# A woven two-stream transformer: another order of the context thread, high halves a slab ahead of low halves, norms in halves, one slab per attention turn, weighted values read from PSUM

## The chip, the cores and the metric

The kernel runs on one core of one Trainium2 chip. The metric is the device time of one execution in microseconds (us). Weights are streamed from HBM during the run; everything else stays in on-chip memory.

## What is computed

Two blocks stand behind one another, each of depth 2, for 256 latent tokens and 256 context tokens of width 1024, all in float32. The reference, cut to what matters:

```python
# first block, per layer l: x = latents, hctx = context, mc / ml = adaptive scales, shifts and gates
x = x + 0.5*gate * swiglu(ada_norm(x, ...), ffn_w_in[l,0], ffn_w_out[l,0])        # "ffn00", "ffn10"
x = x + gate * mixer(ada_norm(x, ...))      # l=0 "even": attention + mLSTM; l=1 "odd": gated linear attention
x = x + 0.5*gate * swiglu(ada_norm(x, ...), ffn_w_in[l,1], ffn_w_out[l,1])        # "ffn01", "ffn11"
# (the same for hctx; in layer 1 the context ends with the mixer's keys and values)
x = rms_norm(x, final_g)                                                           # "final"
# second block, i = 0: "mla" attention, i = 1: "na", a neighbourhood attention
h, hc = x*(1+sc1)+sh1, ctx*(1+csc1)+csh1                                           # "p00", "cp00", "p10", "cp10"
y, yc = mixer(h, hc)
x = _layer_norm(alpha*x + g1*y, ln1_g[i], ln1_b[i])                                # "ln00", "cln00", "ln10"
x = _layer_norm(alpha*x + g2*relu(h2 @ w1)**2 @ w2, ln2_g[i], ln2_b[i])            # "mlp0", "cmlp0", "mlp1"
# (the same for ctx, in i = 0 only: names that begin with c)
```

The adaptive scales come from `silu(c) @ ada_w + ada_b` for two condition vectors, one of the context and one of the latents.

## The kernel before

**Products in three terms.** A float32 product is made of three matmuls in the format fp32r: high x high, high x low, low x high (`products`, lines 2588 to 2596). So each weight slab (128 x 1024, 512 KB) goes through three steps: a DMA into `raw`, a rounding copy on ScalarE into `split_high` (line 1585), and on VectorE `raw - high` into `split_low` (line 2005), which overwrites `raw`. Activations are split in the same way: `h_high` on ScalarE, `h_low` on VectorE (line 2100), and `hidden_high`, `hidden_low` for the feed-forward layers. One slab feeds 24 matmuls of 256 columns (one stream) or 24 of 512 (both streams).

**One order for all engines.** `order()` (line 878) writes out by hand one list of steps, for instance `("up", f, h, ...)`, `("centre", tag, p)`, `("done", slab)`. `schedule()` (line 1064) turns each `done` into the fetch of the slab seven places on and the split of the slab five places on (`SLOTS, LAG = 7, 2`). Then each engine goes through the same list and carries out its own part of every step, in that order; semaphores do the rest. So what stands ahead of a step in the list stands ahead of it in the queue of every engine that has a part in both. A split is one step: ScalarE writes the high half, VectorE waits for it and writes the low half. `raw` and `low` share their memory, `high` has its own, seven buffers each.

**Threads.** Up to the end of the odd mixer both streams are multiplied together (512 columns). From there context and latents run as two threads that are woven: `beside_ffn11` (context mla beside the latents' ffn11), `beside_mla` (the latents' mla beside the context's mlp, "cmlp0"), `beside_mlp0` (the latents' mlp0, with the context's last norm cln01 and the projections of na), `na_steps`, then na_out, ln10, mlp1, ln11 and the store. `weave(pieces, groups)` yields one piece of products, then one group of other steps, in turns; `filled(groups, fill, n)` yields a group and then n pieces; `beside(units, pieces)` gives each attention turn one piece: the turn's steps, the late steps of the piece before (evictions and `done`), the products of the new piece, the scores of the turn.

**Norms.** A layer norm (`layer_norm_groups`, line 657) is: `mean_sum` (TensorE, over an accumulator that GpSimd adds up tile by tile, line 1463), `centre` of eight tiles (VectorE, line 2111, each followed by a square on ScalarE and an add on GpSimd), `sum` (TensorE, line 2646) and `mean` (VectorE, square root on ScalarE, reciprocal, line 2075), `rstd_spread` (TensorE, line 2612), `layer_norm` of eight tiles. `plain_tiles` then makes the scaled and shifted h: `plain` and `plain_put`, eight each, one group of 6 and one of 10.

**Adaptive scales.** 240 blocks of 128 outputs; from the seventh on, VectorE takes for each block two dot products over 1024 inputs, one per condition vector (`ada`, lines 2008 to 2021; the product is line 2019). They are spread over the feed-forward layers: 60 blocks each in ffn00, ffn01, ffn10 and 36 in mlp0. The blocks are loaded through SyncE's queue for odd n and through GpSimd's for even n (lines 1377 and 1450), each at its place in the list.

**Attention of the second block.** A turn u handles 128 queries of a pair of heads: scores in banks 0 to 2, maximum on VectorE, exponential on ScalarE, normalisation on VectorE, transpose by TensorE into banks 3 and 7, copy on ScalarE, and every second turn the weighted values (`mla_weigh`, `na_weigh`) in bank 6. ScalarE copies bank 6 to SBUF (lines 1787 and 1780), then writes the high half from there, and VectorE the low half. In `na_steps` the first five turns have a double piece each, one slab of keys and one of queries, in banks 4 and 5.

**mlp1** has all 32 hidden tiles at once: each of its eight `down` pieces uses four slabs, and the four `done` steps stand together behind the piece, after `add` (line 2208, `down_piece`, line 504).

## Time and profile before

| | |
|---|---|
| median of 3 runs | 3091.31 us (3087.28 to 3095.33) |
| the profiled execution | 3092.23 us, its span 3090.4 us |
| TensorE (PE) busy | 2881.0 us, 93% of the span, 17432 matmuls |
| VectorE (DVE) / ScalarE (ACT) / GpSimd (POOL) busy | 2090.8 / 1279.2 / 331.5 us |
| mean granted TensorE clock | 0.962 of full speed |
| DMA | 467.58 MB, mean 151 GB/s |

A busy TensorE is not TensorE at its peak, since the end of a matmul is modelled. What counts is the number of matmuls in a stretch, against the stretch's length, and the idle time in front of a matmul with what ended it.

### The profile page before, as it was taken

The page shows a single profiled execution, that of the slowest core. Times are in us where ns is not written, and L with a number is a line of the kernel's source. Part 1 is how long each engine was busy: PE and PEld are TensorE (multiplying, and loading weights), DVE is VectorE, ACT ScalarE, POOL GpSimd, SP SyncE. Part 2 cuts the span into 40 slices and gives each one's busy share as a digit, 9 for nine tenths or more (in the row PEclk, how much of TensorE's full clock was granted, in tenths as well). Part 3 has the DMA queues.
Part 4 walks back from the last instruction along what each step waited for, and adds up shares of the span by engine and source line. Part 5 has one row for each costly group of instructions (what it writes and reads, how often), then busy time and mean ns, then how long its engine had stood idle before and what let it go on. Part 6 is the DMA issues. An engine that isn't in the chain of part 4 may idle for free.

```text
span 3090.4 us, 43357 instructions
## 1 busy us (share of the span) xinstructions
PE 2881.0 (93%) x17432; PEld 2508.9 (81%) x17432; DVE 2090.8 (68%) x3510; ACT 1279.2 (41%) x2114; POOL 331.5 (11%) x380
## 2 busy tenths in 40 slices
PE   7999999888999999999999899899999798978998
PEld 6888897547888888888878888898799798966898
DVE  7799756555787857887557655665566799646664
ACT  4222244444322243222355654554555434535553
POOL 0000012222000010000111100221021101200100
PEclk8999999979999999999999999999999898989999
DMA  6666522102555535554322343444255675542453
GB/s 235 225 221 227 176 81 82 38 31 75 177 205 211 178 110 201 202 212 167 101 82 69 130 150 117 150 155 145 76 178 168 215 266 196 184 112 67 130 185 123
DMA packets 141142, 467.58 MB, mean 151 GB/s; under 512 B 26976, under 2 KB 29152, under 8 KB 140432
## 3 DMA queue, kind: packets, MB, share of 16 engines
q1 hardware_dynamic: 125392, 408.20, 39.6%
q0 software_dynamic: 15552, 56.63, 5.2%
q8 instruction: 138, 2.26, 0.3%
q14 instruction: 60, 0.49, 0.0%
HBM read 463.73 MB, written 1.05 MB: 150 GB/s over the span
## 4 chain that ended last, share of the span: by engine, by line
PE 74%; DVE 12%; ACT 8%; issue 3%; DMA 2%; POOL 1%; SPq 0%; ACTq 0%; DVEq 0%; POOLq 0%
PE bank L2593 22%; PE bank L2594 22%; PE bank L2595 22%; DVE sb_split_low L2005 3%; ACT sb_split_high L1585 2%; DVE sb_temp L2019 2%; POOL sb_temp L1463 1%; ACT sb_temp L1910 1%; PE bank L2881 1%; DVE sb_h_low L2092 1%; DMA sb_ada_mlp<-ada 1%; DVE sb_temp L2086 1%; DVE sb_x_res L2208 1%; PE bank L3028 1%; ACT sb_h_high L1656 1%
## 5 line engine op out<-in xcount | busy, mean ns | idle before, releaser
L2593 PE MATMUL bank<-sb_h_high,sb_split_high 128*128 128x256 f32 (+1 forms) x3392 | 1111.6, 328 | 66.2 <-DVE sb_h_low L2100 15.8
L2594 PE MATMUL bank<-sb_h_low,sb_split_high 128*128 128x256 f32 (+1 forms) x3392 | 1092.3, 322 | 0.0
L2595 PE MATMUL bank<-sb_h_high,sb_split_low 128*128 128x256 f32 (+1 forms) x3392 | 1091.7, 322 | 0.0
L2005 DVE TENSOR_TENSOR sb_split_low<-sb_raw,sb_split_high 128x1024 fp32r<-128x1024 f32 x620 | 758.3, 1227 | 267.4 <-ACT sb_split_high L1585 266.1
L1585 ACT ACTIVATE sb_split_high<-sb_raw 128x1024 fp32r<-128x1024 f32 x620 | 644.2, 1051 | 295.5 <-DMA sb_raw<-weights 295.2
L2593 PEld LDWEIGHTS bank<-sb_h_high,sb_split_high 128*128 128x128 f32 x3392 | 659.9, 195 | 131.1 <-DVE sb_h_low L2092 15.9
L2594 PEld LDWEIGHTS bank<-sb_h_low,sb_split_high 128*128 128x128 f32 x3392 | 660.9, 195 | 43.0
L2595 PEld LDWEIGHTS bank<-sb_h_high,sb_split_low 128*128 128x128 f32 x3392 | 660.2, 195 | 43.5
L2019 DVE CUSTOM_DVE_ANT_0 sb_temp<-sb_ada_ffn,sb_cond_ffn 128x1024 bf16<-128x1024 f32 x396 | 465.9, 1220 | 18.8 <-DMA sb_ada_ffn<-ada 10.3
L2593 PE MATMUL bank<-sb_hidden_high_ffn,sb_split_high 128*128 128x512 f32 (+1 forms) x830 | 281.8, 340 | 4.3 <-DVE sb_temp L2186 3.1
L2594 PE MATMUL bank<-sb_hidden_low_ffn,sb_split_high 128*128 128x512 f32 (+1 forms) x830 | 280.1, 338 | 0.0
L2595 PE MATMUL bank<-sb_hidden_high_ffn,sb_split_low 128*128 128x512 f32 (+1 forms) x830 | 280.1, 337 | 0.0
L2208 DVE SCALAR_TENSOR_TENSOR sb_x_res<-bank,sb_gates,sb_x_res 128x256 f32<-128x256 f32 x288 | 132.5, 479 | 152.8 <-PE bank L2595 146.2
L1688 ACT ACTIVATE sb_hidden_high_ffn<-sb_temp 128x512 fp32r<-128x512 f32 (+1 forms) x94 | 52.1, 555 | 344.4 <-DVE sb_temp L2186 344.4
L1675 ACT ACTIVATE sb_temp<-bank 128x256 f32<-128x256 f32 (+1 forms) x158 | 72.4, 458 | 281.5 <-PE bank L2595 281.3
L2593 PEld LDWEIGHTS bank<-sb_hidden_high_ffn,sb_split_high 128*128 128x128 f32 x830 | 157.3, 190 | 23.2 <-DVE sb_temp L2186 3.3
L2594 PEld LDWEIGHTS bank<-sb_hidden_low_ffn,sb_split_high 128*128 128x128 f32 x830 | 157.4, 190 | 18.6
L2595 PEld LDWEIGHTS bank<-sb_hidden_high_ffn,sb_split_low 128*128 128x128 f32 x830 | 157.3, 189 | 18.5
L2593 PE MATMUL bank<-sb_hidden_high_mlp,sb_split_high 128*128 128x256 f32 x512 | 148.2, 289 | 18.1 <-DVE sb_hidden_low_mlp L2198 17.6
L2594 PE MATMUL bank<-sb_hidden_low_mlp,sb_split_high 128*128 128x256 f32 x512 | 146.7, 287 | 0.0
L2595 PE MATMUL bank<-sb_hidden_high_mlp,sb_split_low 128*128 128x256 f32 x512 | 146.7, 287 | 0.0
L2186 DVE TENSOR_TENSOR sb_temp<-sb_temp,bank 128x512 f32<-128x512 f32 (+1 forms) x94 | 55.4, 590 | 133.1 <-PE bank L2595 133.1
(332 smaller groups left out, 3461.2 us busy)
## 6 DMA issues: line engine op xcount, KB each, us to landing
sb_raw<-weights SPq DMA_DIRECT2D x620, 512.0 KB, 3.4
sb_ada_ffn<-ada SPq DMA_DIRECT2D x114, 512.0 KB, 4.5
sb_ada_ffn<-ada POOLq DMA_DIRECT2D x90, 512.0 KB, 3.7
sb_ada_mlp<-ada POOLq DMA_DIRECT2D x18, 512.0 KB, 5.1
sb_ada_mlp<-ada SPq DMA_DIRECT2D x18, 512.0 KB, 5.0
sb_cond_ffn<-cond SPq DMA_DIRECT2D x3, 1024.0 KB, 5.3
sb_na_raw<-na_rpb SPq DMA_DIRECT2D x32, 96.0 KB, 6.0
sb_x_res<-tokens SPq DMA_DIRECT2D x4, 512.0 KB, 8.5
```

The costliest lines, as they stand in the source:

```text
L1463: do.tensor_tensor(acc, other if k == 1 else acc, new, ALU.add).then_inc(*pool.mark("added", (kind, tag, k, p)))
L1585: do.activation(m.high[s % SLOTS][:, :], m.raw[s % SLOTS][:, :], identity).then_inc(*act.mark("split_high", s))
L1656: do.activation(m.hh[:, k, COLS[p]], src, identity).then_inc(*act.mark("h_high", (tag, k, p)))
L1675: do.activation(m.hidden_temp(f, h, p), src, func).then_inc(*act.mark(name, (f, h, p)))
L1688: do.activation(m.hidden[f][i][:, m.hidden_cols(f, p)], m.hidden_temp(f, h, p), identity).then_inc(*act.mark("hidden_high", (f, h, p)))
L2005: do.tensor_tensor(m.low[i][:, :], m.raw[i][:, :], m.high[i][:, :].bitcast(F32), ALU.subtract).then_inc(*dve.mark("split_low", s))
L2019: do.tensor_tensor_reduce(out=m.junk(s), in0=m.ada[f][i][:, :], in1=m.cond[f][:, s, :], scale=1.0, scalar=0.0, op0=ALU.mult, op1=ALU.add, ...
L2186: do.tensor_tensor(temp, temp, src, ALU.mult).then_inc(*dve.mark("hidden_raw", (f, h, p)))
L2208: do.scalar_tensor_tensor(x, m.bank[bank][:, bank_cols(p, s)], m.gates_of(stage)[:, k, s:s + 1], x, ALU.mult, ALU.add).then_inc(*dve.mark( ...
L2593: do.matmul(out, ah, bh, start=start and j == 0, stop=False)
L2594: do.matmul(out, ah, bl, start=False, stop=False)
L2595: last = do.matmul(out, al, bh, start=False, stop=stop and j == len(terms) - 1)
```

## The change

It changes eight things together. (1) `raw` and `low` get eight buffers, `high` six; a slab's high half is still written five `done` steps ahead, its low half only four, and the two are separate steps; the high half also waits for the matmuls of the slab six places back. (2) Layer norms centre and scale in two halves of four tiles, with empty groups between, so that `sum` stands four groups behind `mean_sum`; the plain tiles come in groups of four. Where two fill pieces went with a group (ln00, ln01), one goes. cln01 is spread over twelve pieces of mlp0 instead of eight. (3) Behind odd_out, the norm n12 loses its four warming matmuls, and its `sum` comes after a first projection of the context. (4) Of 64 adaptive blocks (112 to 143, in ffn01, and 208 to 239, in mlp0) only the latents' dot product is taken; the context has no use for its own. All blocks are still loaded. (5) mla's weighted values of two heads share bank 6, and both halves are read from PSUM; VectorE's part (`weigh_put`) stands behind the turn's normalisation. (6) na has one slab per turn; its weighted values go straight into the context's half of h. (7) A `ready` step stands one piece later. (8) The result is stored in four parts of 256 KB.

The diff, cut to its core:

```diff
-SLOTS, LAG = 7, 2
+RAWS, HIGHS = 8, 6
...
-OUT_H = {"odd_out": CTX_PART}
+OUT_H = {"odd_out": CTX_PART, "na_out": CTX_PART}
...
+ADA_OF_LATENTS = ((72 + 5 * DT, 4 * DT), (192 + 2 * DT, 4 * DT))
...
         for k in range(DT - tail if last else DT):
+            body.append(down_piece(f, c, k, p, ring, last))
             if tail and last and k == DT - tail - 1:
                 body.append([("ready", down_slab(f, c, 8 * n - 1))])
-            body.append(down_piece(f, c, k, p, ring, last))
...
-WARM = {("n01", 1): (0, 5), ("n02", 1): (0, 9), ("n10", 1): (0, 5), ("n11", 1): (0, 5), ("n12", 1): (0, 4)}
+WARM = {("n01", 1): (0, 5), ("n02", 1): (0, 9), ("n10", 1): (0, 5), ("n11", 1): (0, 5)}
...
-    return [warm_sum(tag, p, 0) + [("mean_sum", tag, p), ("centre", tag, p)], [], warm_sum(tag, p, 1) + [("sum", tag, p), ("mean", tag, p)],
-            [("rstd_spread", tag, p), ("layer_norm", tag, p)]]
+    first, second = range(0, 4), range(4, DT)
+    return [[], [("mean_sum", tag, p), ("centre", tag, p, first)], [("centre", tag, p, second)], [], [], [("sum", tag, p), ("mean", tag, p)],
+            [("rstd_spread", tag, p), ("layer_norm", tag, p, first)], [("layer_norm", tag, p, second)]]
...
-    return layer_norm_groups(tag, p) + in_groups(plain_tiles(plain, p), (6,))
+    return layer_norm_groups(tag, p) + in_groups(plain_tiles(plain, p), (4, 4, 4) if tag not in NEAR_NORMS else (6,))
...
+        if i > 2 and (i - 2) % per == 0:
+            turn += [("weigh_put", kind, 2 * ((i - 2) // per) - 2), ("weigh_put", kind, 2 * ((i - 2) // per) - 1)]
...
-    for j in range(3):
+    for j in range(4):
         yield from fm_piece("na_k", j, LAT_PART, ring)
         yield from fm_piece("na_q", j, LAT_PART, ring)
...
-    pieces = [both(fm_piece("na_k", j, LAT_PART, ring), fm_piece("na_q", j, LAT_PART, ring)) for j in range(3, 8)]
-    pieces += [*tm_pieces("na_v1", ring), None, None]
+    pieces = [fm_piece(name, j, LAT_PART, ring) for j in range(4, 8) for name in ("na_k", "na_q")]
+    pieces += tm_pieces("na_v1", ring)
...
-    norm = ada_norm_groups("n12", 1)
-    yield from norm[0]
+    sums, spread, *tiles = ada_norm_groups("n12", 1)
     yield from late
-    yield from down[0]
-    yield from weave(norm[1:], down[1:4])
+    yield from weave(down[:6], [sums, [], spread, *tiles])
...
-    yield from filled(layer_and_plain_groups("ln00", "p01", 1), fill, 2)
+    yield from filled(layer_and_plain_groups("ln00", "p01", 1), fill)
...
-    yield from weave(pieces[:8], [[], [], *layer_norm_groups("cln01", 0)])
+    yield from weave(pieces[:12], [[], *layer_norm_groups("cln01", 0)])
...
-    n_split = 0
+    n_high = n_low = HIGHS - 1
     for step in order():
...
+        s = PLACE[step[1]]
+        if step[0] == "done" and s + RAWS < N_SLABS:
+            yield "fetch", s + RAWS
+        ahead = HIGHS - 1 if step[0] == "done" else 0
+        while n_high <= min(s + ahead, N_SLABS - 1):
+            yield "split_high", n_high
+            n_high += 1
+        while n_low <= min(s + max(ahead - 1, 0), N_SLABS - 1):
+            yield "split_low", n_low
+            n_low += 1
...
-        for k in range(DT):
+        for k in range(0, DT, 2):
             wait_for_x(sp, "ln11", k, LAT_PART)
-        do.dma_start(m.out, m.x[:, :, LAT]).then_inc(*sp.mark("stored", "all", step=16))
+            wait_for_x(sp, "ln11", k + 1, LAT_PART)
+            do.dma_start(m.out[:, k:k + 2, :], m.x[:, k:k + 2, LAT]).then_inc(*sp.mark("stored", "all", step=16))
...
+        if s >= HIGHS:
+            act.wait_ge("gemm", s - HIGHS)
+        do.activation(m.high[s % HIGHS][:, :], m.raw[s % RAWS][:, :], identity).then_inc(*act.mark("split_high", s))
...
-            y = m.fm_tile("mla", MLA_QN + hd, p)
-            do.activation(y, m.bank[6][:, 0:NC_TOK], identity).then_inc(*act.mark("weigh_copy", (kind, hd)))
-            act.wait_ge("weigh_copy", (kind, hd))
-            put_high(of(p, "mla_y"), hd, p, y)
+            act.wait_ge("weighed", (kind, hd // 2 * 2 + 1))
+            put_high(of(p, "mla_y"), hd, p, m.weighed(hd))
...
-        for s in range(2):
-            if n > BLOCKS:
+        for s in streams_of_ada(n):
+            if n > BLOCKS and s in streams_of_ada(n - 1):
                 dve.wait_ge("ada_dot", (n - 1, s))
```

## Rows read from the trace of the kernel before

**Rows 1.** The page: busy time of each engine, share of the span, instructions

```profile
PE 2881.0 (93%) x17432; PEld 2508.9 (81%) x17432; DVE 2090.8 (68%) x3510; ACT 1279.2 (41%) x2114; POOL 331.5 (11%) x380
```

**Rows 2.** Stretches: length; PE, PEld, DVE, ACT, POOL busy (count); clock, DMA share, GB/s

```profile
1200.00:1250.00 50.00, 50.00 (x220) 41.13 (x219) 40.19 (x61) 15.59 (x19) 2.65 (x5) 1.00 0.60 204
1710.00:1750.00 40.00, 33.63 (x239) 31.96 (x240) 26.28 (x51) 25.43 (x48) 14.54 (x15) 0.91 0.32 106
1930.00:1985.00 55.00, 45.83 (x345) 44.50 (x345) 34.62 (x61) 33.80 (x59) 21.36 (x22) 0.94 0.42 137
2050.00:2090.00 40.00, 33.66 (x240) 32.88 (x239) 24.27 (x43) 21.79 (x40) 11.23 (x11) 0.87 0.37 127
2275.00:2345.00 70.00, 60.62 (x487) 59.43 (x486) 45.70 (x77) 42.98 (x73) 16.18 (x18) 0.98 0.45 150
2398.00:2633.00 235.00, 199.52 (x1552) 197.07 (x1550) 205.39 (x337) 99.92 (x162) 26.12 (x33) 0.91 0.65 225
...
2683.00:2874.00 191.00, 155.22 (x1070) 131.78 (x1068) 113.33 (x211) 79.59 (x154) 3.26 (x5) 0.92 0.39 106
2895.00:3074.00 179.00, 179.00 (x1510) 178.95 (x1508) 101.76 (x142) 83.16 (x129) 4.44 (x6) 1.00 0.52 168
```

**Rows 3.** What TensorE waited for in the whole span: us, times, longest

```profile
PE bank L2646 <- POOL sb_temp L1463: 21.7, 9, 9.5
PE bank L2593 <- DVE sb_hidden_low_mlp L2198: 17.6, 7, 3.5
PE bank L2593 <- DVE sb_na_k_lat L2218: 16.4, 3, 7.5
...
PE bank L2862 <- ACT sb_mla_ctx L1787: 5.0, 4, 2.7
...
PE bank L2862 <- ACT sb_mla_lat L1787: 2.7, 4, 0.7
```

**Rows 4.** VectorE by line in mlp0 (2400 to 2632 us): count, busy, mean ns, idle before

```profile
L2019 DVE CUSTOM_DVE_ANT_0 sb_temp<-sb_ada_mlp,sb_cond_mlp 128x1024 bf16<-128x1024 f32 x72 | 85.1, 1220 | 8.2 <-DMA sb_ada_mlp<-ada 8.2
```

**Rows 5.** Start of mlp0 in order of time: start, us, engine, line, idle before

```profile
2415.16 2.74 DVE L2111 SCALAR_TENSOR_TENSOR sb_x_res<-bank,sb_x_res 128x256 f32<-128x256 f32 x8
...
2419.55 3.33 POOL L1463 TENSOR_TENSOR sb_temp<-sb_temp,sb_square 128x256 f32<-128x256 f32 x4
...
2422.93 1.02 PE L2646 MATMUL bank<-sb_const,sb_temp 128*128 128x1 f32 x4 [9.51 <-POOL sb_temp L1463]
...
2427.97 1.22 DVE L2019 CUSTOM_DVE_ANT_0 sb_temp<-sb_ada_mlp,sb_cond_mlp 128x1024 bf16<-128x1024 f32 x1 [5.59 <-DMA sb_ada_mlp<-ada]
...
2436.47 1.22 PE L2612 MATMUL bank<-sb_const,sb_stat 128*128 128x128 f32 x4 [7.70 <-DVE sb_stat L2075]
```

**Rows 6.** Stretches of na: the five double turns, the turns after them

```profile
2716.00:2783.00 67.00, 45.71 (x300) 39.88 (x298) 32.56 (x59) 21.60 (x41) 0.00 (x0) 0.85 0.40 99
2783.00:2857.00 74.00, 60.70 (x422) 45.89 (x422) 50.32 (x107) 39.00 (x90) 0.00 (x0) 0.93 0.28 68
```

**Rows 7.** VectorE behind a down piece of mlp1, in order of time

```profile
3051.91 0.48 DVE L2208 SCALAR_TENSOR_TENSOR sb_x_res<-bank,sb_gates,sb_x_res 128x256 f32<-128x256 f32 x1 [5.01 <-PE bank L2595]
3052.31 4.62 DVE L2005 TENSOR_TENSOR sb_split_low<-sb_raw,sb_split_high 128x1024 fp32r<-128x1024 f32 x4
```

**Rows 8.** Two equal waits of TensorE, and the stretch behind each

```profile
1949.68 0.80 PE L2679 MATMUL bank<-sb_temp,sb_const 128*128 128x256 f32 x2 [2.29 <-POOL sb_temp L1463]
...
2278.89 0.70 PE L2679 MATMUL bank<-sb_temp,sb_const 128*128 128x256 f32 x2 [2.29 <-POOL sb_temp L1463]
...
1950.00:1957.00 7.00, 7.00 (x47) 6.92 (x45) 2.74 (x8) 3.07 (x9) 3.98 (x6) 0.76 0.19 68
2279.00:2286.00 7.00, 7.00 (x58) 6.95 (x59) 3.23 (x9) 2.93 (x8) 3.86 (x6) 1.00 0.31 97
```

**Rows 9.** DMA issues of the page: count, KB each, median us to landing; the store in its window

```profile
sb_raw<-weights SPq DMA_DIRECT2D x620, 512.0 KB, 3.4
...
out<-sb_x_res SPq DMA_DIRECT2D x1, 1024.0 KB, 4.8
```

More of the change, by code:

```diff
@@ L680, in beside @@
         late = [step for step in piece if step[0] not in PRODUCTS]
+        if any(step[0] == "tm_copy" and step[1] == "na_v1" for step in late):
+            yield from late
+            late = []
         yield from first
@@ L872, in na_steps @@
         units[2 * t - 1][0].append(("na_bias", t))
-    units[11][0].extend(("na_put", k) for k in range(4))
-    yield from beside(units, pieces)
+    yield from beside(units[:18], pieces)
+    last, _ = units[18]
+    yield from last
     yield from flat(pieces)
@@ L906, in order @@
     yield "scales", "n00"
-    yield "split", 0
+    yield "split_low", 0
     yield "mods", 0, BLOCKS
     first, *tiles = ada_norm_groups("n00", 0)
-    yield from weave([[("split", s)] for s in range(1, SLOTS - LAG)], tiles)
+    yield from weave([[("split_low", s)] for s in range(1, HIGHS - 1)], tiles)
     first, *tiles = ada_norm_groups("n00", 1)
@@ L991, in beside_ffn11 @@
     ring = Ring(0, 4)
[L992 removed]
+    yield from filled([[], down[6]], body)
     yield from mla_front(CTX_PART, ring, body)
@@ L1304, in chunk_of, with streams_of_ada @@
     return max(c for c in range(len(SIZES[f])) if chunk_at(f, c) <= h)
+def streams_of_ada(n):
+    return (1,) if any(first <= n < first + count for first, count in ADA_OF_LATENTS) else (0, 1)
 def ada_stage(n):
```

130 lines of the change are left out of this document (57 added, 73 removed).

## The prediction

> **What bounds the kernel now.** I read the page first. TensorE is busy for 93% of the span [rows 1], so the first guess is TensorE. The stretches say where that holds, and where its granted clock is full. With both streams in one product TensorE has no gap at all, at clock 1.00 (the first stretch of [rows 2]): there an edit for VectorE earns nothing. The same holds in mlp1 (the last stretch of [rows 2]), which also gives the pace of one stream: 179.00 us for 1510 matmuls, 0.1185 us each, 2.84 us for a slab of 24. In the woven part between, the same count takes longer. I price each stretch as its length less 0.1185 us times its matmuls (in order [rows 2]): odd_out and n12 11.7 us too long (40 - 28.3), cln00 14.1, the final norm and p00 11.6, ln00 12.3, mlp0 51.1 (235 - 183.9). For na the form of the matmuls differs, so it is worked out by turns below. The list of TensorE's waits gives the causes [rows 3]: sums that wait for GpSimd's additions (21.7 us), hidden_low in mlp0 (17.6), evictions of na's keys (16.4), and the copies of weighted values (5.0 and 2.7). In mlp0 VectorE is the engine that is full: 205.39 of 235 us [rows 2].
>
> **mlp0, part 4 of the change.** VectorE makes 72 dot products of 1.22 us there [rows 4]. 32 of them go, 32 x 1.22 = 39 us, and VectorE's 205 us become 166, below TensorE's 184: the waits for hidden_low go almost wholly. The 32 in ffn01 earn nothing, since TensorE is full in that kind of stretch [rows 2]. But the start is another matter. mean_sum is followed by eight centrings, squares, and additions of some 0.83 us a tile on GpSimd (3.33 us for 4) [rows 5]; `sum` waited 9.51 us for them. Behind them in GpSimd's queue stands the load of a next adaptive block, so VectorE waited 5.59 us for that DMA, and the spread 7.70 us for VectorE [rows 5]. Now four tiles come ahead of that load and four behind it. The first half is done by about 2419, the load lands some 5 us later, VectorE then has two dot products and two splits before the second half, and `sum` can run at about 2431, when TensorE has been waiting since 2419: a wait of 12 and then one of 2, against 9.5 and 7.7, but with two slabs (5.7 us) more done. So the start gives back only 4 us or so (bounds -3 and 17, all of it). Of the 51 us I take 26 back: 17.6 of waits, about 4 at the start, and 4 of low clock behind them; bounds 10 and 45. All loads remain, 225 GB/s on the mean [rows 2].
>
> **na, part 6.** With a double piece in banks 4 and 5, the next double piece needs both banks, and their evictions stand in VectorE's queue behind the turn's maximum and normalisation. That is the wait on sb_na_k_lat [rows 3]. With one slab a turn, the bank that a piece needs was left two turns earlier. The double turns take 67 us for five [rows 6], 13.4 each; the ten slabs are 28.4 of the 45.71 us that TensorE is busy, which leaves 17.3, some 3.0 to 3.5 for a turn's own matmuls, so 9 a turn would do. Ten slabs of keys and queries are now two ahead and eight in eight turns. VectorE's 32.56 us make 6.5 a double turn; less one split and one eviction, some 1.6, that is 4.9. TensorE has 2.84 + 3.0: I take 5.8. Later turns take 74 us for fourteen, 5.3 each [rows 6]; these keep about their pace. New: 34 us ahead of the turns (8 slabs and v0), 46 for eight turns, 27 for four with v1, 21 and 15 for the last seven, 3 and 13 for what is left of na_out: 159, against 191 [rows 2]. I take 31 back; bounds 14 and 39.
>
> **The norms, parts 2 and 3.** In each of the four stretches the excess is waits on bursts (eight centrings, ten plain tiles in a row) and the clock behind them. `sum` four pieces behind mean_sum is 11.4 us, more than eight additions take. A spread one piece behind its `sum` was still waited for in cln00 and now can be in ln00 and ln01. I take back 5 of 11.7 at n12 (whose four warming matmuls and a wait go, while the wait for the last tiles of cp00 now shows), 9 of 14.1, 8 of 11.6, 8 of 12.3, and 2 for ln01 and ln10 together: 32; bounds 10 and 46.
>
> **Weighted values, part 5.** The two waits go: 5.0 + 2.7 [rows 3], 8 us; bounds 4 and 10 (VectorE's reads of PSUM, which stand in the normalisation's lee).
>
> **Store, part 8.** 1024 KB land in 4.8 us, 512 KB in 3.4 [rows 9]. The last part of 256 KB cannot take longer than the 512: at least 1.4 us less; the straight line gives 2.0, which I take. The worst is 0. The Trainium skill, "DMA: Bandwidth & Descriptors", section "Anatomy of one DMA", gives a fixed cost of about 2.0 us per DMA plus bytes over 436 GB/s: an estimate of 2.6 us for the last part if the four overlap, and of 10.4 if they follow one another, which would turn the 2 us of gain into a loss of some 3. No row of the trace before shows four stores in a row.
>
> **What the split of the splits costs, part 1.** A slab's low half is now made at the `done` four places before it. Where each piece ends one slab, that leaves three slabs of time. In mlp1 a down piece ends four slabs at once, and all four `done` steps stand behind `add`, which waits for the piece's last matmul. So the low half of the next piece's first slab is made only then: 0.40 us from add to the first split and 4.62/4 = 1.16 for it [rows 7], at least 1.6. Two signals come to that, of 0.05 us at the least (the additions end at 2422.88, the sum starts at 2422.93 [rows 5]); with a third of a microsecond for both, 1.9 us of waiting at seven piece borders (the first is fed by the ups), 13 us. The clock: of two equal waits of 2.29 us one was followed by 0.76 over 7 us, which is 0.24 x 7 = 1.7 us lost to time at 1.2 instead of 2.4 GHz, the other by 1.00, full speed [rows 8]. I count it at two of seven, 4 us: 17 us lost, bounds 12 and 26. Elsewhere VectorE is spared waiting for the high half of the same slab; I count the gain as nothing and let the range have it, with the new wait of ScalarE for the slab six back (long done where it is asked). The later `ready` is covered by a piece of products. The Trainium skill, "TensorE: Matmul & The Clock Gate", section "HAM oscillation", has a kernel whose wait in every step of a loop put the array back on half clock every time; by it the clock would be paid at all seven borders.
>
> **The sum.** Back: 26 + 31 + 32 + 8 + 2 = 99. Lost: 17, and 8 for waits that come in place of those removed (VectorE's 166 of 184 us in mlp0 leave it little room), bounds 0 and 25. Net 74. The profiled execution took 3092.2, 0.9 above the median of the runs, so 3092.2 - 74 = 3018.
>
> **Rivals.** (a) The forecast, 3018, own range 3000 to 3034: 0.40. (b) The clock falls at every border of mlp1: 7 x 1.7 = 12 instead of 4, so 3026. For it stands the first pair of [rows 8], against it the second: 0.10. (c) The chains, not the bursts, set the pace: in mlp0 the loads (GpSimd's block behind the additions) keep VectorE waiting and only 10 come back, in na the turn is bound by maximum, exponential, normalisation at some 7 us instead of 5.8, and 15 come back; 3018 + 16 + 16 = 3050. For it: 5.59 us of waiting on a load [rows 5] and turns of 5.3 with little more than half a slab in each [rows 6]. 0.22. (d) The waits go wholly: mlp0 gives 45, na 37, the norms 38, nothing comes in their place: 3018 - 19 - 6 - 6 = 2987, or 2979 with the 8. For it: VectorE has room in every woven stretch but mlp0 [rows 2]. 0.18. (e) Slower: the later low halves reach TensorE late in the whole woven part, not in mlp1 alone. The place is VectorE's queue wherever it runs more than three slabs behind; the price is one slab, 2.84 us, at each such place; it decides from (99 - 17)/2.84 = 29 places on; with 35 of them it gives 3092 - 99 + 17 + 99 = 3109. Against it: VectorE is busy for about two thirds of most of these stretches [rows 2]. 0.04. (f) The gains are there but each is eaten by the next wait, and little is left, 3085 to 3100: 0.06, the rest.
>
> **How the numbers follow.** 0.3%, some 9 us, is about what a measurement of this kernel can tell from no change. Faster by more than that takes (a) to (d) and a sliver of (f): 0.91; within: 0.05; slower: 0.04. The range goes from the near end of (d) to beyond (c), 2986 to 3060, and leaves out about 2 in 10.
>
> **What would show it.** In the changed profile: mlp0's stretch near 209 us for its 1552 matmuls, with line 2019's successor at 40 dot products and no wait for hidden_low above 2 us; `sum` of cln01 still waiting some 10 us; na's stretch near 160; no wait of a weigh for its copy; in mlp1 seven waits on sb_split_low of 1.9 us and 192 to 196 us for the 1510 matmuls. I would be wrong in the mechanism if mlp1 showed no such waits, or if VectorE were still full in mlp0.

## The result, and the profile after

The changed kernel takes 2977.0 us (median of four runs, 2976.8 to 2977.8) against 3090.7 for the kernel before: a ratio of 0.963 with a 95% interval of 0.9615 to 0.9648, 114 us less. My forecast was 3018, and 2977 lies below the low end of my range, 2986. The direction was right and the size wrong, by 41 us. Two of four later runs of the changed kernel, at 3502 and 3504 us and a granted clock of 0.74, were in a slower state and count nowhere below.

The busy times of the page, TensorE first (busy, share, instructions), and below them VectorE and ScalarE:

```profile
PE 2838.8 (95%) x17424; PEld 2478.5 (83%) x17424; DVE 2010.1 (68%) x3382; ACT 1275.3 (43%) x2092; POOL 338.6 (11%) x380
```

VectorE did 80.7 us less (64 dot products of 1.22 us are 78 of them). TensorE's busy time fell by 42 us with only 8 matmuls fewer [rows 1]. Most of that is clock: the mean granted clock over the span rose from 0.962 to 0.978, and what the low clock took from TensorE while it was busy fell from 88.8 to 52.4 us. Its idle time in front of matmuls fell from 197.8 to 126.7 us.

The stretches, with the columns of [rows 2], cut so that each holds about as many matmuls as before: n12, cln00, the final norm and p00, ln00, mlp0, na and mlp1.

```profile
1702.00:1738.00 36.00, 30.77 (x237) 30.15 (x238) 25.22 (x46) 23.63 (x45) 13.92 (x15) 0.95 0.37 126
1904.00:1948.00 44.00, 41.67 (x342) 40.98 (x341) 30.83 (x53) 27.66 (x48) 17.08 (x17) 1.00 0.52 171
2013.00:2044.00 31.00, 29.55 (x244) 28.94 (x243) 22.02 (x42) 19.99 (x39) 9.55 (x10) 1.00 0.49 165
2216.00:2283.00 67.00, 61.60 (x504) 60.33 (x503) 47.26 (x83) 42.87 (x73) 22.38 (x22) 1.00 0.49 164
2336.00:2541.00 205.00, 189.17 (x1553) 188.41 (x1552) 168.79 (x272) 100.84 (x162) 26.37 (x33) 0.96 0.72 258
2590.00:2746.00 156.00, 144.46 (x1054) 123.79 (x1054) 111.60 (x210) 75.12 (x144) 1.99 (x3) 0.97 0.48 126
2767.00:2961.00 194.00, 181.76 (x1510) 180.33 (x1510) 102.74 (x143) 86.16 (x129) 4.43 (x6) 1.00 0.45 152
```

By the pace of [rows 2], 0.1185 us a matmul, the excess is 7.9, 3.5, 2.1 and 7.3 us in the four norm stretches (11.7, 14.1, 11.6, 12.3 before), 21.0 in mlp0 (51.1), and in mlp1 it is 15.1 where there was none. The granted clock is at 1.00 in three of the six woven stretches (all but mlp1); before it was in none.

TensorE's waits in the whole span (us in total, times, longest):

```profile
PE bank L2601 <- DVE sb_split_low L2015: 15.0, 9, 2.0
PE bank L2654 <- POOL sb_temp L1483: 14.8, 6, 12.2
PE bank L2601 <- DVE sb_h_low L2110: 13.0, 10, 2.5
PE bank L2638 <- DMA sb_ada_ffn<-ada: 12.9, 3, 9.2
PE bank L2620 <- DVE sb_stat L2085: 8.1, 5, 3.2
...
PE bank L2601 <- DVE sb_hidden_low_mlp L2208: 0.4, 1, 0.4
```

Of the rows that led my list [rows 3], hidden_low went from 17.6 to 0.4, sb_na_k_lat and both copies of weighted values are gone, and the wait for GpSimd's additions went from 21.7 to 14.8, nearly all of it one wait of 12.2. The new first row is sb_split_low, and seven of its nine waits lie in mlp1.

What I had misjudged shows in another row: VectorE's own waits. The first row is of the page of before and is not among those that the prediction uses; the second answers to it in the changed kernel (count, busy, mean ns, then VectorE's idle time just before and what ended it).

```profile
L2005 DVE TENSOR_TENSOR sb_split_low<-sb_raw,sb_split_high 128x1024 fp32r<-128x1024 f32 x620 | 758.3, 1227 | 267.4 <-ACT sb_split_high L1585 266.1
```

```profile
L2015 DVE TENSOR_TENSOR sb_split_low<-sb_raw,sb_split_high 128x1024 fp32r<-128x1024 f32 x620 | 758.3, 1232 | 13.6 <-ACT sb_split_high L1603 13.6
```

VectorE stood 266 us, in 230 waits, with a low half next in its queue, waiting for ScalarE to make the high half of the very same slab. Now it is 13.6. Everything queued behind (evictions, additions, norms) stood there with it. The idle time as such did not go: VectorE is idle for 965 us of the span against 1000 before, and its waits for TensorE's results grew (the largest two rows from 165.7 and 133.1 to 206.6 and 200.8). What changed is what it waits for.

To place the gain in time I matched the two traces by the weight products (15,594 in each, in the same order but for a few pieces) and took the difference of the time between equal counts. In us less than before: up to 1703 us of the changed kernel 7.6; odd_out and n12 5.2; ffn11 with mla's context half 13.6; cln00 10.7; final norm and p00 9.9; mla's latent half 9.4; ln00 5.3; mlp0 32.7; ln01 and cna -1.0; na 34.6; mlp1 -14.9; the tail after the last product 2.2. The sum is 115.3, the difference of the two spans (3090.4 and 2975.1).

### The profile page after: what moved, and what is told of

The parts are those of the page before. It is cut to its first block and busy times, and to the rows that moved or that the text cites. A ratio compares the mean times of both kernels' runs of the same rounds, so it can differ in the third digit from the quotient of the medians.

```text
span 2975.1 us, 43424 instructions
## 1 busy us (share of the span) xinstructions
PE 2838.8 (95%) x17424; PEld 2478.5 (83%) x17424; DVE 2010.1 (68%) x3382; ACT 1275.3 (43%) x2092; POOL 338.6 (11%) x380
## 5 line engine op out<-in xcount | busy, mean ns | idle before, releaser
L2015 DVE TENSOR_TENSOR sb_split_low<-sb_raw,sb_split_high 128x1024 fp32r<-128x1024 f32 x620 | 758.3, 1232 | 13.6 <-ACT sb_split_high L1603 13.6
L2029 DVE CUSTOM_DVE_ANT_0 sb_temp<-sb_ada_ffn,sb_cond_ffn 128x1024 bf16<-128x1024 f32 x364 | 429.6, 1219 | 24.0 <-DMA sb_ada_ffn<-ada 15.3
L2196 DVE TENSOR_TENSOR sb_temp<-sb_temp,bank 128x512 f32<-128x512 f32 (+1 forms) x94 | 55.5, 590 | 202.3 <-PE bank L2603 200.8
L2601 PE MATMUL bank<-sb_hidden_high_mlp,sb_split_high 128*128 128x256 f32 x512 | 144.2, 282 | 12.6 <-DVE sb_split_low L2015 12.2
L1461 POOL DMA_DIRECT2D sb_ada_ffn<-ada x90 | 47.8, 531 | 844.0 <-DVE sb_ada_col L2029 844.0
```

The source lines that it names most:

```text
L1461: lane.do.dma_start(m.ada[f][i][:, :], m.w["ada"][n, :, :]).then_inc(*lane.mark(ada_signal(n), n, step=16))
L2015: do.tensor_tensor(m.low[i][:, :], m.raw[i][:, :], m.high[s % HIGHS][:, :].bitcast(F32), ALU.subtract).then_inc(*dve.mark("split_low", s))
L2029: do.tensor_tensor_reduce(out=m.junk(s), in0=m.ada[f][i][:, :], in1=m.cond[f][:, s, :], scale=1.0, scalar=0.0, op0=ALU.mult, op1=ALU.add, ...
L2196: do.tensor_tensor(temp, temp, src, ALU.mult).then_inc(*dve.mark("hidden_raw", (f, h, p)))
L2601: do.matmul(out, ah, bh, start=start and j == 0, stop=False)
```

## The experiments

Unless said otherwise each kernel is the changed one with the edit shown, its time a median of four runs, and "against the changed kernel" means against 2977.0. "Stage" figures are read from the one profiled execution of each kernel, matched by weight products as above, so they need not add up to the difference of the medians: the profiled run was the fastest of four for before_staggered (3063.9) and the slowest for done_before_add (2964.4) and all_dots (3003.2). Part of the scatter between kernels is not the edit's: more on that at one_store.

**The low half beside the high half (low_beside_high).**

```diff
-        while n_low <= min(s + max(ahead - 1, 0), N_SLABS - 1):
+        while n_low <= min(s + ahead, N_SLABS - 1):
```

> The changed kernel with one edit: the low half of a slab is made at the same `done` as its high half, five places ahead, as before the change; the eight raw buffers stay. Measured so far: 2977.0 us for the changed kernel; mlp1 took 15 us longer than before, with seven waits on sb_split_low of up to 1.9 us (12.2 in all), and the two attention stages of mla took some 27 us less than before, of which my prediction priced 7.7. Theory A: the order of the splits is what costs in mlp1 (the low halves behind `add`) and what gains in mla (the lone split_low waits of 3.6 and 2.6 us there, and the clock behind them): then mlp1 gives 15 us back, mla loses some 10 to 15, and the whole is 2970 to 2980. Theory B: the gain in mla comes from the weighted values read from PSUM and has nothing to do with the splits: then mla stays, mlp1 gives 15 back, and the whole is 2962 to 2966. Theory C (rival): the seven waits come from the buffers and not from the order; then they stay and the whole is 2977.

3001.9 us (ratio to before 0.9713, 0.9698 to 0.9727): 24.9 more. mlp1 got its 14.9 back and has no such wait; all else lost 39 us by stage (up to n12 10.1, of which 6.3 ahead of odd_out, where both streams are multiplied together; mla's context half 7.8; cln00 3.7; final norm 2.1; mla's latent half 1.7; ln00 4.2; mlp0 2.5; na 6.7; the rest small). VectorE's waits:

```profile
DVE sb_split_low L2015 <- ACT sb_split_high L1603: 269.9, 244, 7.9
```

The waiting is back whole, so it is the order that makes it. TensorE's idle time is 138.2 us against 126.7, although the 12.2 of mlp1 are gone: 24 of the 39 us are idle time, and the rest is busy time at the same matmuls, that is mostly clock (0.972 against 0.978). None of my three theories had the sum: A had mlp1 right and mla nearly (9.5 us lost in its two halves, 10 to 15 said), but not the 30 us that other stages lost. B and C are wrong.

How such a wait reaches TensorE is seen in the kernel before, at 1797 us (start, us, engine, idle before):

```profile
1796.82 1.99 ACT L1585 ACTIVATE sb_split_high<-sb_raw 128x1024 fp32r<-128x1024 f32 x2
...
1797.90 1.23 DVE L2005 TENSOR_TENSOR sb_split_low<-sb_raw,sb_split_high 128x1024 fp32r<-128x1024 f32 x1 [0.79 <-ACT sb_split_high L1585]
1799.04 0.75 DVE L2478 COPY sb_mla_kv<-bank 128x256 f32<-128x256 f32 x2
1799.56 0.36 PE L2593 MATMUL bank<-sb_h_high,sb_split_high 128*128 128x256 f32 x1 [3.55 <-DVE sb_split_low L2005]
```

ScalarE was late with two slabs, VectorE waited 0.79 us for the first, and TensorE, whose next matmul needed that slab, waited 3.55 us until its low half was made (it ended at 1799.12).

**Part 1 alone on the kernel before (before_staggered).** Seven buffers as before, high halves five places ahead, low four. The diff is cut to its core.

```diff
-            last = step[1] + (SLOTS - LAG if step[0] == "done" else 0)
-            while n_split <= min(last, N_SLABS - 1):
+            ahead = SLOTS - LAG if step[0] == "done" else 0
+            while n_high <= min(step[1] + ahead, N_SLABS - 1):
+                yield "split_high", n_high
+                n_high += 1
+            while n_split <= min(step[1] + max(ahead - 1, 0), N_SLABS - 1):
...
```

> The kernel before with one part of the change alone: ScalarE makes the high half five places ahead, VectorE the low half four places ahead, in the seven buffers it has. My prediction priced this part at 17 us lost (mlp1's seven borders) and nothing gained: 3108 by it. Theory A: the part is worth the same on the old schedule as undoing it cost on the new one, 24.9 us net (40 gained where both streams' work is woven, 15 lost in mlp1): 3064 to 3069. Rival B: the other parts are what leaves VectorE the room to profit; in mlp0, where it is busy 205 of 235 us, and at the bursts of the norms the freed waiting is filled at once: 3075 to 3095. Rival C: on the old schedule, where VectorE's waits stall TensorE more often, it is worth more than 25: 3050 to 3063.

3066.3 us (ratio 0.9921, 0.9906 to 0.9936), 24.0 less than the 3090.3 of the kernel before in the same sitting. That is theory A: the part is worth about the same on either schedule. That 24.0 and 24.9 agree to 1 us is luck, since each is good to 3 to 5. In the profiled execution, 28.6 us shorter than that of the kernel before, mlp1 loses 17.4 us and all else gains 46, 9 of them ahead of odd_out and 7.4 in mlp0, where undoing the part on the new schedule cost only 2.5. VectorE's waits for high halves are 13.9 us here.

**The order or the eighth buffer (seven_staggered).** `RAWS, HIGHS = 7, 7`, high halves still five ahead, low four.

> The changed kernel with the buffers of before (seven raw, seven high) and its new order of the splits (high five places ahead, low four). Measured so far: with the low half beside the high one and eight raw buffers 3001.9, 24.9 us more than the changed kernel; all stages but mlp1 lose some 40 us together, mlp1 gains 14.9; VectorE waits 270 us for ScalarE's high halves there (266 before the change), 13.6 in the changed kernel. Theory A: it is the order alone, since VectorE no longer stands behind ScalarE: then this kernel is 2977, at most 2980. Rival B: a part of it is the eighth raw buffer, which lets a load start one slab earlier; then the raw tiles are late in places, and the time lies between 2980 and 3000, with waits of sb_split_high on the DMA.

2980.5 us (2977.4 to 2982.8), 3.5 more, with no stage more than 2.6 longer. VectorE waits 13.9 us for high halves, as in the changed kernel. ScalarE now waits for the loads of the raw slabs, as B has it, but nobody waits for ScalarE (idle before, and what ended it):

```profile
L1603 ACT ACTIVATE sb_split_high<-sb_raw 128x1024 fp32r<-128x1024 f32 x620 | 646.8, 1051 | 322.0 <-DMA sb_raw<-weights 317.0 <-PE bank L2603 5.0
```

It is the order; the eighth raw buffer, and six `high` buffers instead of seven, bring nothing that these runs resolve.

**The low halves ahead of `add` (done_before_add).**

```diff
-    steps = [("down", f, c, k, p, bank), ("add", f, (f, c, k), k, p, bank), *part_done(f, p, *done)]
+    steps = [("down", f, c, k, p, bank), *part_done(f, p, *done[:-1]), ("add", f, (f, c, k), k, p, bank), *part_done(f, p, *done[-1:])]
```

> The changed kernel with one edit: in a down piece that ends four slabs, the first three `done` steps stand ahead of `add`, so that VectorE makes those low halves while TensorE is still in the piece. If the low half behind `add` is the cause of the seven waits in mlp1, they go (12.2 us) and with them the low clock behind some of them, 15 us in all, while everything else stays: 2962 (2960 to 2965). If the cause is that four slabs of weights end at once and the fetches or the high halves are late, the waits stay and the time is 2977. A loss is possible where the add of another kernel stage is now held up behind a split that waits for its high half: then 2980 or more, with new waits on sb_x_res.

2960.7 us (ratio 0.958, 0.9566 to 0.9595), 16.3 less, nearly all of it in mlp1 (14.9 by stage). First a border of mlp1 in the changed kernel (the first one: the addition, the low halves behind it and TensorE's wait), then the same border here.

```profile
2867.08 0.48 DVE L2218 SCALAR_TENSOR_TENSOR sb_x_res<-bank,sb_gates,sb_x_res 128x256 f32<-128x256 f32 x1 [8.38 <-PE bank L2603]
2867.48 4.62 DVE L2015 TENSOR_TENSOR sb_split_low<-sb_raw,sb_split_high 128x1024 fp32r<-128x1024 f32 x4
...
2868.85 0.36 PE L2601 MATMUL bank<-sb_hidden_high_mlp,sb_split_high 128*128 128x256 f32 x1 [1.80 <-DVE sb_split_low L2015]
```

```profile
2859.91 4.62 DVE L2015 TENSOR_TENSOR sb_split_low<-sb_raw,sb_split_high 128x1024 fp32r<-128x1024 f32 x4
2869.51 0.48 DVE L2218 SCALAR_TENSOR_TENSOR sb_x_res<-bank,sb_gates,sb_x_res 128x256 f32<-128x256 f32 x1 [4.98 <-PE bank L2603]
```

There VectorE sits idle 8.38 us and then makes four halves in a row, too late for the first. Here three of them are made in that idle time (the first of the four in the row is that of the slab before, due there in both kernels), and TensorE has no wait on sb_split_low in all of mlp1. The cause at the borders is shown, and this is the first kernel that beats both.

**Weighted values copied again, in mla (weigh_copies).** ScalarE copies them to sb_mla_ctx and sb_mla_lat, both reads come from there, and each head has the whole bank to itself again; VectorE's part stays at its new place, behind the turn's normalisation.

> The changed kernel with the weighted values of mla copied by ScalarE to sb_mla_ctx or sb_mla_lat and read from there, as before the change (na keeps reading PSUM). Theory A, by my prediction's term: the waits of the weigh products for the copies come back, 5.0 + 2.7 us, and the whole is 2984 to 2986. Theory B: those waits were also what put the clock down behind them and what held the low splits back; then all that the two mla stages gained beyond the order of the splits comes back, 15 to 27 us, and the whole is 2992 to 3004. Rival: the copies were waited for only because VectorE's part stood at another place of the turn; with the puts at the end of the turn nothing comes back and it is 2977 to 2980.

2987.2 us, 10.1 more: 4.3 and 3.6 in mla's two halves, the rest spread. The waits for the copies are back as two rows:

```profile
PE bank L2871 <- ACT sb_mla_ctx L1799: 3.5, 4, 1.2
PE bank L2871 <- ACT sb_mla_lat L1799: 2.7, 4, 0.7
```

My term, 8, holds; theory B does not: the mla stages gained 23.0 and this part is 7.9 of it.

**All dot products (all_dots).** `ADA_OF_LATENTS = ()`: 64 more, whose results nothing uses.

> The changed kernel with the dot products of the adaptive blocks made for both streams again (32 more in ffn01, 32 more in mlp0; what they write is not used). mlp0 took some 210 us against 235 before, all but 15.4 us of waits of its first blocks gone. Theory A (mine): VectorE's time in mlp0 goes from 166 to 205 us beside 184 us of TensorE, the waits for hidden_low come back, and mlp0 takes 15 to 22 us more, ffn01 nothing: 2992 to 2999. Rival: the later splits or the spread norms were what freed mlp0, and the 64 products cost little: 2977 to 2982. Second rival: ffn01 also pays, since the low halves are now made later: 3005 or more.

2999.0 us, 21.9 more; mlp0 takes 23.4 more by stage, every other stage 1.7 or less, ffn01 0.0, so the 32 products dropped there earned nothing, as forecast. mlp0's stretch is this, and its waits on hidden_low are back (9.5 us, 6 times):

```profile
2336.00:2564.00 228.00, 197.82 (x1551) 194.25 (x1549) 203.70 (x336) 99.96 (x163) 26.03 (x32) 0.93 0.66 231
```

VectorE is at 204 of 228 us again and the clock at 0.93 instead of 0.96. TensorE's idle time grew by 14 of the 23 us and its busy time by 8.7 (197.82 against 189.17); the latter goes with the clock.

**Two slabs a turn in na (na_double).** Three of eight keys and queries ahead, then `both(...)` for five, and two empty places, as before.

> The changed kernel with na's keys and queries two slabs a turn again (three of eight ahead, five double pieces in banks 4 and 5). The stretch of na became 34.6 us shorter with the change, of which the run with the low halves beside the high ones gave 6.7 back. Theory A (mine): the pairing in two banks cost the rest, by evictions that stand behind the turn's normalisation: then 22 to 30 us come back, all in na: 2999 to 3007, with waits on sb_na_k_lat of some 15 us. Rival: most of it was the low halves and the weighted values, and the pairing costs only the 3 to 10 us that the waits' excess over a turn makes: 2980 to 2987.

3003.9 us, 26.9 more; 22.2 of it in na, 4.2 in mlp0, which the edit does not touch. The row of before is back:

```profile
PE bank L2601 <- DVE sb_na_k_lat L2228: 16.6, 3, 7.7
PE bank L2601 <- ACT sb_na_k_lat L1718: 4.9, 2, 3.2
```

The weighted values of na, which also lost their copy with the change, were tried in no run.

**The norms whole and early (norms_whole).** One centring and one normalisation a norm, `sum` two groups behind, plain tiles in sixes, two pieces a group in ln00 and ln01; the final norm in one part, p00 in fours as before.

> The changed kernel with the norms of the woven stretches in one part each and early, as before (cln00, cln01, ln00, ln01, the final norm and p00; n12 keeps its new order). Measured gains of these stages: cln00 10.7, final norm and p00 9.9, ln00 5.3, mlp0 32.7, of which the late low halves give 3.7, 2.1, 4.2 and 2.5 and the dot products of mlp0 23.4. Theory A: what is left is the norms': 7.0 + 7.8 + 1.1 + 6.8 = 23, so 2997 to 3002. Rival B: the parts are not separate; without the freed VectorE the bursts cost more, now they cost less, and only 8 to 15 come back: 2985 to 2992. In both the mlp0 part would be a wait of the spread for VectorE (7.7 us before).

2996.6 us, 19.5 more: cln00 6.8, final norm and p00 8.1, mla's latent half 2.8, mlp0 4.2, ln00 0.1, ln01 with cna -1.0. Just short of theory A (2997 to 3002), far from B. The spread of cln01 waits 7.9 us for VectorE again (7.7 before).

**One store (one_store), the same once more (one_store_again), and the changed kernel once more (after_again).**

```diff
-        for k in range(0, DT, 2):
+        for k in range(DT):
             wait_for_x(sp, "ln11", k, LAT_PART)
-            wait_for_x(sp, "ln11", k + 1, LAT_PART)
-            do.dma_start(m.out[:, k:k + 2, :], m.x[:, k:k + 2, LAT]).then_inc(*sp.mark("stored", "all", step=16))
+        do.dma_start(m.out, m.x[:, :, LAT]).then_inc(*sp.mark("stored", "all", step=16))
```

> The changed kernel with one store of all eight tiles at the end, as before the change. From the last product of weights to the end of the span it was 16.2 us before and 14.1 with four stores. If the four stores are what made that difference, it is 16.2 again and the time 2979; if the norm's end is what became shorter, it stays at 14.1 and the time at 2977.

> The kernel with one store once more. Theory A (scatter between sittings): anywhere from 2977 to 2988, and not with the same extra time in mlp0, cna, na and mlp1. Theory B (its own time, by the clock's answer to the same waits): 2985 to 2988 again, with the same stages longer. The tail is 16.3 us in both.

> The changed kernel once more, unchanged. Theory A: the 6.8 us that one_store lost outside its tail are scatter between one placing of the program and the next, or between hours on the chip: then this run may lie anywhere from 2974 to 2985. Theory B: a program's time is its own to 1 us: then 2976 to 2978.

2986.6 us, then 2981.7 in another sitting; the changed kernel came to 2976.2 and 2973.7 in that sitting (two runs; ratio 0.9628, 0.9609 to 0.9647). From the last weight product to the end of the span it is 16.3 us with one store and 14.1 with four: 2.2 us, the only thing that the edit can reach. The other 7 us of the first sitting lie in mlp0 (1.4), cna (1.7), na (1.6) and mlp1 (2.7). mlp1 there has the same seven waits, 12.2 us in all, but the clock stands at 0.98, not 1.00:

```profile
2774.00:2970.00 196.00, 183.77 (x1496) 182.10 (x1496) 102.55 (x144) 84.87 (x127) 4.44 (x6) 0.98 0.45 148
```

Ten of the profiles have these seven waits, 12.2 us in all each time. Behind them the granted clock fell to half in none of the seven in three profiles (the changed kernel, one_store_again, norms_whole), in one in three (after_again, na_double, all_dots) and in two in four (one_store, seven_staggered, before_staggered, weigh_copies): 11 falls for 70 waits, each 1.7 us lost, and mlp1's 1505 weight products take 193.5 to 196.8 us with it. One of the falls, in one_store:

```profile
2874.00:2877.00 3.00, 3.00 (x16) 3.00 (x15) 2.22 (x2) 0.00 (x0) 0.00 (x0) 0.50 0.00 0
```

So the same schedule gives times that differ by some 5 us between sittings, in part by the clock's answer to equal waits, and single runs of one kernel in one sitting differ by up to 9 us (2950.6 to 2960.0 for sum_later_sp). A single term above is good to 3 to 5 us and not better; the 3.5 of seven_staggered is inside that.

**The start of mlp0.** cln01's `sum` waits 12.2 us. The rows say why: GpSimd adds the first squares, then issues a block's load, VectorE waits for that block, and the second four tiles are behind it.

```profile
2357.06 0.57 POOL L1461 DMA_DIRECT2D sb_ada_mlp<-ada  x1
...
2361.59 1.23 DVE L2029 CUSTOM_DVE_ANT_0 sb_temp<-sb_ada_mlp,sb_cond_mlp 128x1024 bf16<-128x1024 f32 x1 [5.13 <-DMA sb_ada_mlp<-ada]
...
2369.68 1.01 PE L2654 MATMUL bank<-sb_const,sb_temp 128*128 128x1 f32 x4 [12.24 <-POOL sb_temp L1483]
```

Five kernels, all with the early low halves (alone 2960.7), take it up. The waits given are TensorE's.

sp_loads_early_done, all adaptive blocks loaded by SyncE and none by GpSimd:

> Two edits to the changed kernel: the first three `done` steps of a down piece ahead of `add` (alone: 2960.7 us, mlp1's seven waits gone), and all adaptive blocks loaded by SyncE, none by GpSimd. In cln01 `sum` waits 12.2 us for GpSimd's additions and the spread 3.2 for VectorE, because GpSimd issues a block's load behind its first additions and VectorE waits 5.1 us for that block ahead of the second centring. Theory A: without that load the second half of the norm comes some 5 to 6 us earlier, and 5 to 9 us are gained: 2952 to 2956. Rival B: VectorE's own queue (dot products and splits between the halves) sets the place of `sum`; then nothing is gained, 2959 to 2961. Rival C: SyncE's queue, with loads waiting for a free block, holds the weights' loads back: then the raw tiles are late and the time is 2965 or more.

2958.0 us; the wait of `sum` is 7.5.

sum_later, `sum` three pieces later:

> Two edits to the changed kernel: the early `done` steps of the down pieces (alone 2960.7) and, in cln01 beside mlp0, `sum` and all behind it three pieces later; GpSimd goes on loading its blocks. Three more pieces are 3 to 6 us of products ahead of `sum`, so the wait of 12.3 us for GpSimd's additions shrinks to some 6 to 9 and, if the clock fell in it, a little more comes back: theory A 2953 to 2957. Rival B: the products in the added pieces themselves wait for VectorE, whose queue is what is late (hidden_low); then the wait only changes its name and the time is 2959 to 2962.

2959.5 us; the wait for the additions is gone, and 11.4 us on sb_split_low, 8.3 of them at one place, stand in its place.

sum_later_sp, both:

> The same with all adaptive blocks loaded by SyncE (with the early `done` steps and SyncE's loads, without the later `sum`: 2958.0, the wait for the additions 7.5 us). Theory A: three pieces more take 3 to 6 us of those 7.5, and the spread's 3 to 4 us shrink too: 2950 to 2954. Rival B, as above: VectorE's queue is late and the wait changes its name: 2957 to 2960.

2952.9 us (2950.6 to 2960.0; ratio 0.9558, 0.9543 to 0.9573); mlp0 takes 4.0 less by stage than in the changed kernel, and 8.2 us of waiting on sb_split_low remain, 4.8 of them at one place.

loads_ahead, each block of mlp0 loaded four blocks ahead of its dot product, by the engine that loads it now:

```diff
+def loads_at(n):
+    first, count = FFN["mlp0"][1:3]
+    if n < first:
+        return [n]
+    early = [n, n + 2] if n < first + 2 else []
+    return early + [n + 4] * (n + 4 < first + count)
...
-            load_ada(m, pool, n)
+            for at in loads_at(n):
+                load_ada(m, pool, at)
```

> Two edits: the early `done` steps (alone 2960.7) and, in mlp0, the load of an adaptive block issued four blocks ahead of its dot product instead of at its place, on the same engines. In the changed kernel VectorE waits 5.1 us for a block's load ahead of the second centring, the load having been issued behind GpSimd's additions and 3.6 us away from its data. Theory A: that wait goes, the second half of the centrings comes 4 to 5 us earlier, `sum` waits 7 to 8 instead of 12.3, and VectorE keeps up in the rest of mlp0: 2953 to 2957. Rival B: GpSimd's eight additions and ScalarE's squares set `sum`'s place, the load is hidden: 2959 to 2962. Rival C: earlier loads hold SyncE or GpSimd in a wait for a free block, and weights come late: over 2965.

2957.7 us; the wait is 7.9, mlp0 takes 3.8 less by stage, and VectorE's wait for blocks fell from 21.6 us, 13 times, to 2.3, twice:

```profile
PE bank L2664 <- POOL sb_temp L1493: 7.9, 1, 7.9
PE bank L2630 <- DVE sb_stat L2095: 4.2, 1, 4.2
DVE sb_temp L2039 <- DMA sb_ada_mlp<-ada: 2.3, 2, 2.0
```

loads_ahead_later, with `sum` three pieces later:

> The same with `sum` three pieces later (with the early `done` steps alone 2959.5, where the wait had moved to sb_split_low, 8.3 us at one place, since VectorE stood waiting for a block's load). Theory A: with the loads ahead VectorE doesn't stand, the 8.3 us at sb_split_low go to 0 to 2, and the `sum` wait stays away: 2946 to 2951, faster than all so far. Rival B: the wait for VectorE stays wherever it is put, since VectorE has more work at the start of mlp0 than TensorE: 2956 to 2960.

2954.5 us (2950.6 to 2957.1; ratio 0.9561, 0.9547 to 0.9575); 7.6 us of waiting on sb_split_low, where theory A said 0 to 2.

So the load accounts for some 4 to 5 us of the 12.2. The rest did not go with it: put `sum` later, and the wait takes another name. That this rest is VectorE's and GpSimd's own work at that place is the likely reading, and no run takes such work away there. All five kernels lie within 7 us of each other, near the scatter; sum_later_sp and loads_ahead_later are the fastest, some 23 us below the changed kernel, and I don't rank them. Of those 23 us, 16 are those of done_before_add.

## Why the prediction was wrong

**The step that failed.** It is in "What the split of the splits costs": "Elsewhere VectorE is spared waiting for the high half of the same slab; I count the gain as nothing and let the range have it." That part, priced at 17 lost, measured 24 to 25 gained, on both schedules: 39 back by stage on the new one (33 of them where work is woven, 6 ahead of it), against 15 lost in mlp1. What I put at nothing without a number was the largest term of all, and my bounds for the part, 12 to 26 lost, had no gain in them either. The error of this one step, 42 us, is as large as the whole miss (41). The other parts were 17 too high together (99 against the 82 that undoing them one by one gives), and the 8 for new waits and 7 that no single part shows offset 15 of that. The row that points to it stood on the page of before: 266 us of VectorE waiting for ScalarE. I read TensorE's waits and VectorE's busy share and saw room at two thirds busy; but while an engine stands in front of one step, nothing behind that step is done, however little the engine is busy. The row gives the place and not the price:

```profile
DVE sb_split_low L2005 <- ACT sb_split_high L1585: 155.3, 139, 5.2
```

That is the woven part of the kernel before, from 1703 to 2895 us, where 33 us came back; 94.0 us of such waits lie ahead of it, where 6 came back (9 on the old schedule). The price has to be sought in TensorE's own waits that end with VectorE's work: in the woven part of the list of before sb_h_low has 15.8 + 1.6, sb_ctx_temp 8.8 and sb_split_low 6.1, 32 us, and there is the clock behind them. That is a size to start from, not a bound.

**mlp1's borders: right, to a tenth.** Forecast: seven waits on sb_split_low of 1.9 us, 13 us, stretch 192 to 196. Found: 12.2 in seven (six of 1.8 to 1.9, one of 1.4), stretch 194. The clock term was 4 (two of seven borders); ten profiles had none to two falls, 1.1 on the mean, of the 1.7 us that I had priced. The changed kernel's own profile has none, and still 2.9 us remain beside the waits (15.1 - 12.2). 1.7 of them lie at the same borders, for which I had no term: at six of them, from the last matmul's start before the wait to the first one's behind it are 2.08 to 2.14 us, and then 0.19 to the next, where the pace is 0.12, so each border costs 0.24 more than the idle time shown. Rival (b), a fall at every border, is wrong. The Trainium skill, "TensorE: Matmul & The Clock Gate", section "HAM oscillation", tells of a kernel where a wait at every step put the array back on half clock each time. Those waits were longer, some 3 to 5 us by the page, and I should not have carried the effect over to waits of 1.9; here the clock fell at 11 of 70 borders.

**mlp0: 26 forecast, 32.7 by stage, 30 by stretch** (205 us for 1553 matmuls; I had said 209). VectorE is at 168.8 us (166 said), 40 dot products, hidden_low 0.4. At the start I said a wait of 12 and one of 2: it was 12.2 and 3.2, for the reasons given. The dot products alone are 22 to 23. TensorE's busy time fell by 10.4 us (199.52 to 189.17) as the clock rose from 0.91 to 0.96, where my term was 4.

**na: 31 forecast, 34.6**, 156 us (160 said); the pairing alone is 22 to 27 by na_double, and 6.7 of the stage are the splits'. The other 5.7 no run takes apart.

**The norms: 32 forecast, 31.1 minus 1.0 by stage** (n12 5.2 for 5, cln00 10.7 for 9, final norm 9.9 for 8, ln00 5.3 for 8, ln01 and cna -1.0 for 2). But the sum is right by offset: norms_whole gives only 19.5 for this part. Some 14 us of these stages (3.8 + 3.7 + 2.1 + 4.2) belong to the splits. I had read the excess of a stretch and given all of what could go to the norms in it. n12's new order was not tried alone; what is left for it is 5.2 - 3.8.

**Weighted values: 8 forecast, 10.1** (7.9 in mla). The mla stages gained 23.0 in all; the other 15 I had nowhere. Undone one at a time, the splits' order gives 9.5 of them and the norms 2.8.

**Store: 2.0 forecast, 2.2.** Each of the four parts landed 2.6 us after its issue, and they were issued within 3.4 us, so they overlap:

```profile
out<-sb_x_res SPq DMA_DIRECT2D x4, 256.0 KB, 2.6
```

By the Trainium skill, "DMA: Bandwidth & Descriptors", section "Anatomy of one DMA", the estimate was 2.6 us for one part; the trace agrees, though the section gives its fit for DMAs that GpSimd issues and SyncE issues these.

**"8 for waits that come in place of those removed"**: little of it came. Beside the waits forecast in mlp1 and cln01, the largest that the list of before does not have are in na: 2.4 us on sb_na_q, and 5.8 on an exponential (sb_temp L1920), where it was 3.6.

**Before the woven part** I forecast nothing and 7.6 us came. 6.3 us of it went again with the low halves beside the high ones, and the order alone gave 9 on the old schedule, though 3 us of such figures are inside the scatter that the last stretch of it shows (3.2 us between two profiles of the changed kernel).

**Do the parts add up?** Undone one at a time: 24.9 + 26.9 + 19.5 + 21.9 + 10.1 + 2.2, and 1.4 for n12, are 107 of 114. In the sum the parts hardly overlap, though stage by stage they do (mlp0, at before_staggered); 7 us are within what six scatters leave.

Rival (d), 2979 to 2987, came nearest to the time, and its mechanism (the waits go wholly, nothing in their place) is half of the truth; I gave it 0.18 and closed the range at its edge. It too lacked the 40.

## What to carry to other kernels

Read not only what the bounding engine waits for but what its helpers wait for at the head of their queues: a helper that is 68% busy and stands 266 us in front of one step can be a late helper. How much of it counts is told only by who waits for what stands behind: here some 40 us of the 266 came back. Where two engines make halves of the same thing, let the second one work on what the first finished a step ago; that was worth 24 us here, twice. And put the work for the next piece ahead of the step that waits for the end of this one: three `done` steps ahead of one addition gave 16 us more.

## What the hardware showed that I had not expected

Seven waits of 1.4 to 1.9 us in mlp1, one about every 13 us, left the granted clock at 1.00 in one_store_again and at 0.98 in one_store, which is the same kernel; over ten profiles it fell behind 11 of 70 such waits, and one fall costs 1.7 us. And the clock was a large share of what the shorter waits gave: in cln00 it rose from 0.94 to 1.00 and TensorE's busy time fell by 4.2 us (45.83 to 41.67, 345 and 342 matmuls) of the 11 that the stretch gained; at the final norm it rose from 0.87 to 1.00 and busy time fell by 4.1 of 9 us.
